# A two-layer decoder trunk in float32 on one core: the moves of transposed blocks by way of DRAM issued from GpSimd's queue instead of SP's

## The chip, the core and the metric

The kernel runs on one core of a Trainium2 chip. The core has TensorE (PE in the profile: matmuls, with PEld for the loading of weights into the array), VectorE (DVE), ScalarE (ACT), GpSimd (POOL) and SyncE (SP), which here does nothing but issue DMAs, and 16 DMA engines that all queues share. The metric is the time of one execution on the device in microseconds (us), the median of several runs.

## The reference

Two layers over 256 positions of width 2048, all in float32. Layer 0 mixes with retention heads and a gated linear recurrence, layer 1 with attention (16 heads), and each is followed by a gated MLP with a causal convolution of width 3 between up-projection and activation. Cut to what matters here:

```python
def conv_ffn(h, w_up, conv_w, conv_b, w_down):
    u = causal_dwconv(h @ w_up, conv_w, conv_b)
    gate, val = jnp.split(u, 2, axis=-1)
    return (jax.nn.gelu(gate) * val) @ w_down

for l in range(DEPTH):
    hn = rmsnorm(x, norm_mix[l])
    x = x + (even_mixer(hn, ...) if l % 2 == 0 else odd_mixer(hn, ...))
    x = x + conv_ffn(rmsnorm(x, norm_ffn[l]), ffn_w_up[l], ffn_conv_w[l], ffn_conv_b[l], ffn_w_down[l])
```

## The kernel before

**Weights in chunks.** Every projection is cut into blocks of 512 output columns, and a block into chunks of 256 rows, 512 KB each. There are 784 chunks. SP loads a chunk into one of four buffers `raw` (line 314), ScalarE copies it into `w_hi` (line 471), VectorE writes the remainder into `w_lo` (line 1099), and TensorE multiplies with both, so that float32 precision is kept. A load waits for `lo_ready` of the chunk four before it, ScalarE for the landing and for TensorE's end with the chunk four before (`chunk_used`). SP, ScalarE, VectorE and TensorE all walk through the same list of chunks; work between the chunks is placed by hand at a stage, the number of the chunk in the block behind which it stands.

**Blocks that come out transposed.** In most blocks TensorE computes positions by columns (`chunk_rows`, `chunk_values`: 12 matmuls a chunk, lines 837 to 839 and 855 to 857), while what follows needs columns by positions. VectorE transposes such a block from PSUM into `cross` in squares of 32 by 32 (`STREAM_TRANSPOSE`, two instructions: lines 1258 and 1259 in the up-projection, 1203, 1204, 1114, 1115, 1227 and 1547 elsewhere). The squares still have to change partitions. That is done by a move through DRAM: `put` writes `cross` in four pieces of 128 KB into `turn_line` (line 334, semaphore `put_out`), and `fetch` reads the 512 KB back into `h` (line 339, semaphore `moved`), once all four have landed. There are 69 such moves: 6 in the input projections of each layer, 3 in each output projection, 22 in each up-projection, 3 and 4 in the down-projections (the last four turn the residual x).

**The up-projection**, where 44 of the 69 are, has 22 blocks of 8 chunks in each layer, two to a turn (gate and value); the first turn stands apart, the other ten are a loop on every engine. For a block, VectorE transposes behind chunk 2 of the next block, waits for `moved` behind its chunk 7 and scales h (line 1265). ScalarE makes the first tap of the convolution behind chunk 0 of the block after that (line 534), VectorE the two others behind chunks 1 and 2 (lines 1272 and 1279), and then comes the transpose of the next block. `cross`, `turn_line` and `h` exist once, so one move must be over, and h be used up, before the next.

**Where the moves are issued.** All on SP, in the list of weight loads. In the up-projection `put` stands behind the load of chunk 6 and `fetch` behind the load of chunk 0 of the next block. In the input and output projections and the first layer's down-projection the places are like these, written out by hand. GpSimd loads a few constants at the start, the bias table once layer 0 is finished (line 445), and writes three of the four output blocks (line 449); it waits otherwise.

Of the kernel before, what the change touches and what calls it, by code (L numbers as in the profile page):

```python
# [21 lines left out]
P = 128  # L22
D = 2048
S = 256
# [3 lines left out]
NB = 512  # L28
BT = NB // P
CT = 2  # L30
RING = 4
# [6 lines left out]
PAIRS = D_FF // NB  # L38
SQ = 32
QUADS = P // SQ  # L40
OUTB = D // NB
ROWS = OUTB - 1
MOVED_QK = 3
# [4 lines left out]
HEADS, HEAD_DIM = 16, 128  # L48
# [22 lines left out]
MOVED_IN = (2, 3, 4, 5, 7, 8)  # L71
# [9 lines left out]
LAYER_TURNS = (INB * KC + OUTB * KC + 2 * PAIRS * KC + OUTB * FC) // RING  # L81
# [49 lines left out]
def build(nc, x_t, params, w_gates, rope, decay, rel_bias, buckets, identity,  # L131
# [3 lines left out]
    phases = (Phase(0), Phase(1))  # L135
# [63 lines left out]
    bias, _ = work("bias", [P, HEADS, S])  # L199
# [11 lines left out]
    bias_line = nc.dram_tensor("bias_line", (HEADS, 3 * P), F32, kind="Internal").ap()  # L211
# [27 lines left out]
    bias_loaded = sem("bias_loaded")  # L239
# [65 lines left out]
    def _(sp):  # L305
# [7 lines left out]
            src = w[bass.ds(rows * (CT * P), CT * P), cols].rearrange("(t p) n -> p t n", p=P)  # L313
            sp.dma_start(raw[:, s, :, :], src).then_inc(landed[s], 16)

        def put(n):

            sp.wait_ge(acc_drained, n + 1)
            write_quads()

        def put_x(k):

            sp.wait_ge(x_flipped, k + 1)
            write_quads()

        def put_qk(k):

            sp.wait_ge(qk_flipped, k + 1)
            write_quads()

        def write_quads():
            for i in range(QUADS):
                dst = turn_line[:, i, :].rearrange("(g c) n -> c g n", g=QUADS)
                sp.dma_start(dst, flip_quads[i * SQ:(i + 1) * SQ, :, :]).then_inc(put_out, 16)

        def fetch(k):

            sp.wait_ge(put_out, 16 * QUADS * (k + 1))
            sp.dma_start(h_quads[:, :, :], turn_line[:, :, :]).then_inc(moved, 16)

        for ph in phases:
            l = ph.layer
            for b, (_, _, col) in enumerate(ODD_BLOCKS if l else EVEN_BLOCKS):
                for c in range(KC):
                    if (l, b, c) == (0, 0, 0):
                        for u, landing in enumerate((tile_landed, landed[0])):
                            sp.dma_start(raw[:, 0, u, :], w_in[0][u * P:(u + 1) * P, col:col + NB]).then_inc(landing, 16)
                        continue
                    if (l, b, c) == (0, 0, 5):
                        sp.dma_start(par[:, 4 * KT:], params[:, 4 * KT:]).then_inc(const_loaded, 16)  # L350
                    load(w_in[l], ph.q_in + 2 * b, c, slice(col, col + NB), c)
                    if l and b >= 2 and b % 3 != 1 and b < 3 * MOVED_QK + 1:
                        k = 2 * ((b - 2) // 3) + (b % 3 == 0)
                        if c == 2:
                            put_qk(k)
                        if c == 4:
                            fetch(ph.m_in + k)
                    if l == 0 and b - 2 in MOVED_IN and c == 0:
                        fetch(MOVED_IN.index(b - 2))
                    if l == 0 and b - 1 in MOVED_IN and c == 6:  # L360
                        put(b - 1)
                    if (l, b) == (0, 0) and c in (1, 3, 4):
                        j = (1, 3, 4).index(c) + 1
                        part = slice(j * BT, (j + 1) * BT)
                        sp.dma_start(x_res[:, part, :], x_t[:, part, :]).then_inc(x_loaded[j], 16)
            for b in range(OUTB):
                for c in range(KC):
                    load(w_out[l], ph.q_out + 2 * b, c, slice(b * NB, (b + 1) * NB), MIX_ORDER[l][c])
                    if b >= 2 and c == 0:
                        fetch(ph.m_out + b - 2)  # L370
                    if b and c == 6:
                        put(ph.n_out + b - 1)
            for half in range(2):
                for c in range(KC):
                    load(w_up[l], ph.q_up + 2 * half, c, slice(half * D_FF, half * D_FF + NB), c)
                    if half == 0 and c == 0:
                        fetch(ph.m_up - 1)
                    if half and c == 6:
                        put(ph.n_up)
            with sp.Fori(1, PAIRS) as j:  # L380
                for half in range(2):
                    for c in range(KC):
                        load(w_up[l], ph.q_up + 4 * j + 2 * half, c, bass.ds(j * NB + half * D_FF, NB), c)
                        if c == 0:
                            fetch(ph.m_up + 2 * j + half - 2)
                        if c == 6:
                            put(ph.n_up + 2 * j + half - 1)
            for b in range(OUTB):
                cols = slice(b * NB, (b + 1) * NB)
                for c in range(FC) if b == 0 else DOWN_HEAD:  # L390
                    load(w_down[l], ph.q_down, FC * b + c, cols, c)
                    if b == 0 and c in (0, 8):
                        fetch(ph.m_down - 2 + c // 8)
                    if b == 0 and c == 6:
                        put(ph.n_down - 1)
                    if l and (b, c) == (0, 18):
                        put_x(0)
                    if l and (b, c) == (0, 20):
                        fetch(ph.m_down)
                    if l and b and c == 7:  # L400
                        put_x(b)
                    if l and b and c == 9:
                        fetch(ph.m_down + b)
                    if b and l == 0 and c == 6:
                        put(ph.n_down + b - 1)
                    if b and l == 0 and c == 8:
                        fetch(ph.m_down + b - 1)
                if b == 0:
                    continue
                with sp.Fori(*DOWN_TURNS) as t:  # L410
                    for i in range(RING):
                        load(w_down[l], ph.q_down + t, FC * b + i, cols, RING * t + i)
                for c in DOWN_TAIL:
                    load(w_down[l], ph.q_down, FC * b + c, cols, c)
# [7 lines left out]

    @block.gpsimd
    def _(pool):
        nc.gpsimd.memset(ones[:, :], 1.0).then_inc(consts_set, 1)

        pool.wait_ge(consts_set, 1)
# [11 lines left out]
        pool.dma_start(bias_line[:, :], line[0:HEADS, :]).then_inc(line_stored, 16)  # L439
        pool.wait_ge(line_stored, 16)  # L440

        pool.wait_ge(chunk_used, RING * LAYER_TURNS)

        hankel = bass.AP(bias_line.tensor, 0, [[1, P], [3 * P, HEADS], [1, S]])
        pool.dma_start(bias[:, :, :], hankel).then_inc(bias_loaded, 16)
        for b in range(OUTB - 1):

            pool.wait_ge(acc_drained, phases[1].n_down + b + 1)
            pool.dma_start(out_t[:, :, b * NB:(b + 1) * NB], x_nat[:, b, :, :]).then_inc(stored, 16)
        pool.wait_ge(stored, 16 * (OUTB - 1))  # L450


# [1305 lines left out]
```

## Time and profile before

| | us |
|---|---|
| median of three runs (2203.89 to 2205.47) | 2203.9 |
| the profiled execution | 2206.2 |
| its span, first to last instruction | 2204.3 |

| engine | busy us | share of the span |
|---|---|---|
| PE | 2197.0 | 100% |
| PEld | 1831.2 | 83% |
| DVE | 1509.0 | 68% |
| ACT | 1156.0 | 52% |
| POOL | 7.7 | 0% |

The granted clock of TensorE is 1.00 over the whole span. The DMA engines are busy for 71% of it and move 493 MB at 224 GB/s; 263808 of the 265777 packets come from SP's queue. Matmuls overlap in the profile: one has a duration of 0.39 us, and one begins every 0.23 us. So a pause of TensorE is read from the distance of two starts, not from the idle time alone.

### The profile page before, as it was taken

The page shows a single profiled execution, that of the slowest core. Times are in us where ns is not written, and L with a number is a line of the kernel's source. Part 1 is how long each engine was busy: PE and PEld are TensorE (multiplying, and loading weights), DVE is VectorE, ACT ScalarE, POOL GpSimd, SP SyncE. Part 2 cuts the span into 40 slices and gives each one's busy share as a digit, 9 for nine tenths or more (in the row PEclk, how much of TensorE's full clock was granted, in tenths as well). Part 3 has the DMA queues.
Part 4 walks back from the last instruction along what each step waited for, and adds up shares of the span by engine and source line. Part 5 has one row for each costly group of instructions (what it writes and reads, how often), then busy time and mean ns, then how long its engine had stood idle before and what let it go on. Part 6 is the DMA issues. An engine that isn't in the chain of part 4 may idle for free.

```text
span 2204.3 us, 28925 instructions
## 1 busy us (share of the span) xinstructions
PE 2197.0 (100%) x10046; PEld 1831.2 (83%) x10046; DVE 1509.0 (68%) x1923; ACT 1156.0 (52%) x1442; POOL 7.7 (0%) x17
## 2 busy tenths in 40 slices
PE   9999999999999999999999999999999999999999
PEld 8888888888888888888888888888888888888887
DVE  7877766777777776645566665576777777766444
ACT  6554455555655565444455555555555555554443
POOL 0000000000000000000000000000000000000000
PEclk9999999999999999999999999999999999999999
DMA  7766667777787777666676675567777777777664
GB/s 271 220 218 194 208 204 225 226 233 245 233 256 226 250 230 248 222 206 204 205 238 193 211 235 161 191 213 240 232 245 231 252 230 242 232 244 244 208 222 161
DMA packets 265777, 493.25 MB, mean 224 GB/s; under 512 B 18549, under 2 KB 53893, under 8 KB 265568
## 3 DMA queue, kind: packets, MB, share of 16 engines
q1 hardware_dynamic: 263808, 485.96, 70.5%
q0 software_dynamic: 1456, 5.65, 0.7%
q8 instruction: 51, 0.84, 0.2%
q10 hardware_dynamic: 432, 0.56, 0.1%
q14 instruction: 30, 0.25, 0.0%
HBM read 453.80 MB, written 38.30 MB: 223 GB/s over the span
## 4 chain that ended last, share of the span: by engine, by line
PE 80%; DMA 7%; DVE 6%; issue 3%; ACT 2%; SPq 1%; DVEq 0%; ACTq 0%
PE ps L855 15%; PE ps L856 15%; PE ps L857 15%; PE ps L837 8%; PE ps L839 8%; PE ps L838 8%; PE ps L814 6%; DMA h<-turn_line 5%; PE ps L818 3%; DMA turn_line<-cross 1%; DVE h L1265 1%; ACT w_hi L471 1%; DVE w_lo L1099 1%; DVE pad_g L1279 1%; DVE pad_g L1272 1%
## 5 line engine op out<-in xcount | busy, mean ns | idle before, releaser
L1099 DVE TENSOR_TENSOR w_lo<-raw,w_hi 128x1024 fp32r<-128x1024 f32 x783 | 948.4, 1223 | 561.5 <-ACT w_hi L471 535.1
L471 ACT ACTIVATE w_hi<-raw 128x1024 fp32r<-128x1024 f32 x783 | 813.9, 1056 | 680.8 <-PE ps L839 252.6
L855 PE MATMUL ps<-w_hi,xs 128*128 128x512 f32 x2048 | 799.0, 390 | 0.4 <-DVE w_lo L1099 0.4
L857 PE MATMUL ps<-w_hi,xs 128*128 128x512 f32 x2048 | 796.9, 389 | 0.0
L856 PE MATMUL ps<-w_lo,xs 128*128 128x512 f32 x2048 | 796.8, 389 | 0.0
L855 PEld LDWEIGHTS ps<-w_hi,xs 128*128 128x128 f32 x2048 | 384.4, 188 | 80.8 <-DVE w_lo L1099 1.3
L857 PEld LDWEIGHTS ps<-w_hi,xs 128*128 128x128 f32 x2048 | 384.4, 188 | 79.8
L856 PEld LDWEIGHTS ps<-w_lo,xs 128*128 128x128 f32 x2048 | 384.5, 188 | 79.1
L837 PE MATMUL ps<-w_hi,act 128*128 128x512 f32 x808 | 314.8, 390 | 1.0 <-DVE w_lo L1099 1.0
L838 PE MATMUL ps<-w_lo,act 128*128 128x512 f32 x808 | 314.4, 389 | 0.0
L839 PE MATMUL ps<-w_hi,act 128*128 128x512 f32 x808 | 314.4, 389 | 0.0
L837 PEld LDWEIGHTS ps<-w_hi,act 128*128 128x128 f32 x808 | 151.7, 188 | 32.7 <-DVE w_lo L1099 1.4
L839 PEld LDWEIGHTS ps<-w_hi,act 128*128 128x128 f32 x808 | 151.7, 188 | 31.6
L838 PEld LDWEIGHTS ps<-w_lo,act 128*128 128x128 f32 x808 | 151.7, 188 | 31.4
L814 PE MATMUL ps<-act,w_hi 128*128 128x512 f32 (+1 forms) x304 | 95.4, 395 | 0.0
L1265 DVE TENSOR_TENSOR h<-h,rstd 128x1024 f32<-128x1024 f32 x44 | 53.9, 1226 | 44.3 <-DMA h<-turn_line 43.4
L814 PE MATMUL ps<-xs,w_hi 128*128 128x512 f32 x256 | 80.9, 397 | 1.7 <-DVE w_lo L1616 1.3
L818 PEld LDWEIGHTS ps<-act,w_lo 128*128 128x128 f32 x304 | 57.1, 188 | 13.5
L542 ACT ACTIVATE act<-pad_v 128x1024 f32 (+1 forms) x22 | 23.4, 1063 | 80.1 <-DVE pad_v L1289 80.1
L534 ACT ACTIVATE pad_v<-h,par 128x256 f32<-128x256 f32 x88 | 45.8, 592 | 35.1 <-DVE h L1265 35.1
L818 PE MATMUL ps<-act,w_lo 128*128 128x256 f32 (+1 forms) x304 | 59.7, 278 | 0.0
L818 PEld LDWEIGHTS ps<-xs,w_lo 128*128 128x128 f32 x256 | 48.1, 188 | 11.3
(206 smaller groups left out, 1138.3 us busy)
## 6 DMA issues: line engine op xcount, KB each, us to landing
raw<-w_up SPq DMA_DIRECT2D x352, 512.0 KB, 4.6
raw<-w_in SPq DMA_DIRECT2D x191, 512.0 KB, 4.3
raw<-w_down SPq DMA_DIRECT2D x176, 512.0 KB, 4.6
turn_line<-cross SPq DMA_DIRECT2D x276, 128.0 KB, 2.5
h<-turn_line SPq DMA_DIRECT2D x69, 512.0 KB, 5.9
raw<-w_out SPq DMA_DIRECT2D x64, 512.0 KB, 4.6
bias<-bias_line POOLq DMA_DIRECT2D x1, 2048.0 KB, 11.0
x_res<-x_t SPq DMA_DIRECT2D x3, 512.0 KB, 7.2
```

Source lines behind the costliest of these rows:

```text
L471: act_f(w_hi[:, s, :, :], raw[:, s, :, :], ACT.Copy).then_inc(hi_ready, 1)
L534: ins = act_f(by_quad(pad[:, t, 0:S]), h_tiles[:, :, t, :], ACT.Identity, scale=w, bias=b)
L814: return mm(ps[:, 4 * group + m, :], w_hi[:, s, u, m * P:(m + 1) * P], rhs, start=first and u == 0, stop=False)
L818: return mm(ps[:, 4 * group + m, 0:S], w_lo[:, s, u, m * P:(m + 1) * P], rhs[:, 0:S], start=False, stop=last and u == CT - 1)
L837: mm(out, x_hi, w_hi[:, s, u, :], start=first and u == 0, stop=False)
L838: mm(out, x_hi, w_lo[:, s, u, :], start=False, stop=False)
L839: ins = mm(out, x_lo, w_hi[:, s, u, :], start=False, stop=last and u == CT - 1)
L855: mm(out, x_hi, w_hi[:, s, u, :], start=first and u == 0, stop=False)
L856: mm(out, x_hi, w_lo[:, s, u, :], start=False, stop=False)
L857: ins = mm(out, x_lo, w_hi[:, s, u, :], start=False, stop=last and u == CT - 1)
L1099: tt(w_lo[:, s, :, :], raw[:, s, :, :], w_hi[:, s, :, :].bitcast(F32), ALU.subtract).then_inc(lo_ready, 1)
L1265: tt(h_tiles, h_tiles, scale, ALU.mult).then_inc(normed, 1)
```

## The change

SP keeps the weight loads, three loads of x, the parameters and the last output writes. Its `put`, `put_x`, `put_qk`, `write_quads` and `fetch` move to GpSimd word for word, but for the engine. GpSimd gets a list of its own, in which each move is a wait for the transpose, four writes, a wait for `put_out` and the read. The bias table and the output writes are placed in that list. The other engines' programs are the same.

```diff
         def load(w, q, c, cols, rows):
...
-        def put(n):
-
-            sp.wait_ge(acc_drained, n + 1)
-            write_quads()
...
-        def fetch(k):
-
-            sp.wait_ge(put_out, 16 * QUADS * (k + 1))
-            sp.dma_start(h_quads[:, :, :], turn_line[:, :, :]).then_inc(moved, 16)
...
                 for half in range(2):
                     for c in range(KC):
                         load(w_up[l], ph.q_up + 4 * j + 2 * half, c, bass.ds(j * NB + half * D_FF, NB), c)
-                        if c == 0:
-                            fetch(ph.m_up + 2 * j + half - 2)
-                        if c == 6:
-                            put(ph.n_up + 2 * j + half - 1)
...
     @block.gpsimd
     def _(pool):
+        def put(n):
+
+            pool.wait_ge(acc_drained, n + 1)
+            write_quads()
...
+        def write_quads():
+            for i in range(QUADS):
+                dst = turn_line[:, i, :].rearrange("(g c) n -> c g n", g=QUADS)
+                pool.dma_start(dst, flip_quads[i * SQ:(i + 1) * SQ, :, :]).then_inc(put_out, 16)
+
+        def fetch(k):
+
+            pool.wait_ge(put_out, 16 * QUADS * (k + 1))
+            pool.dma_start(h_quads[:, :, :], turn_line[:, :, :]).then_inc(moved, 16)
...
-        pool.wait_ge(chunk_used, RING * LAYER_TURNS)
-
-        hankel = bass.AP(bias_line.tensor, 0, [[1, P], [3 * P, HEADS], [1, S]])
-        pool.dma_start(bias[:, :, :], hankel).then_inc(bias_loaded, 16)
-        for b in range(OUTB - 1):
-
-            pool.wait_ge(acc_drained, phases[1].n_down + b + 1)
-            pool.dma_start(out_t[:, :, b * NB:(b + 1) * NB], x_nat[:, b, :, :]).then_inc(stored, 16)
+        for ph in phases:
+            l = ph.layer
+            if l:
+                pool.wait_ge(chunk_used, RING * LAYER_TURNS)
+                hankel = bass.AP(bias_line.tensor, 0, [[1, P], [3 * P, HEADS], [1, S]])
+                pool.dma_start(bias[:, :, :], hankel).then_inc(bias_loaded, 16)
+                for k in range(2 * MOVED_QK):
+                    put_qk(k)
+                    fetch(ph.m_in + k)
+            else:
+                for k, b in enumerate(MOVED_IN):
+                    put(b)
+                    fetch(k)
+            for b in range(ROWS):
+                put(ph.n_out + b)
+                fetch(ph.m_out + b)
+            for j in range(PAIRS):
+                for half in range(2):
+                    put(ph.n_up + 2 * j + half)
+                    fetch(ph.m_up + 2 * j + half)
+            if l:
+                put_x(0)
+                fetch(ph.m_down)
+            for b in range(ROWS):
+                if l:
+                    put_x(b + 1)
+                    fetch(ph.m_down + b + 1)
+                    pool.wait_ge(acc_drained, ph.n_down + b + 1)
+                    pool.dma_start(out_t[:, :, b * NB:(b + 1) * NB], x_nat[:, b, :, :]).then_inc(stored, 16)
+                else:
+                    put(ph.n_down + b)
+                    fetch(ph.m_down + b)
```

SP's program in layer 0's up-projection loop, the kernel before: the loads of chunks 6, 7 and 0 and the move among them. (ISA and REGISTER_ALU are SP's own waits and address sums; a load is the row with `raw`.)

```order
L314 DMA raw<-w_up 128x2x512
L318 REGISTER_ALU
L334 DMA turn_line<-cross 32x4x256 [waits acc_drained]
L334 DMA turn_line<-cross 32x4x256 x3
L312 REGISTER_ALU
L314 ISA [waits lo_ready]
L314 DMA raw<-w_up 128x2x512
L312 ISA
L314 ISA [waits lo_ready]
L314 DMA raw<-w_up 128x2x512
L338 ISA
L339 DMA h<-turn_line 128x1024 [waits put_out]
```

The same place in the kernel after, on SP:

```order
L314 DMA raw<-w_up 128x2x512
L312 REGISTER_ALU
L314 ISA [waits lo_ready]
L314 DMA raw<-w_up 128x2x512
L312 ISA
L314 ISA [waits lo_ready]
L314 DMA raw<-w_up 128x2x512
```

Only the loads are left, each behind its own wait. On GpSimd in the kernel after, two moves of the same up-projection (the loop is written out there):

```order
L380 DMA turn_line<-cross 32x4x256 [waits acc_drained]
L380 DMA turn_line<-cross 32x4x256 x3
L385 DMA h<-turn_line 128x1024 [waits put_out]
L380 DMA turn_line<-cross 32x4x256 [waits acc_drained]
L380 DMA turn_line<-cross 32x4x256 x3
L385 DMA h<-turn_line 128x1024 [waits put_out]
```

Writes and read stand together there, with no load between them. The end of GpSimd's program after, in layer 1's down-projection:

```order
L380 DMA turn_line<-cross 32x4x256 [waits x_flipped]
L380 DMA turn_line<-cross 32x4x256 x3
L385 DMA h<-turn_line 128x1024 [waits put_out]
L432 DMA out_t<-x_res 256x1x512 [waits acc_drained]
L1689 UNCONDITIONAL_BRANCH [waits stored]
```

An output write, which had GpSimd's queue to itself, now stands behind a move.

## Rows read from the trace of the kernel before

**Rows 1.** The page's first part: busy time, share of the span, instructions.

```profile
PE 2197.0 (100%) x10046; PEld 1831.2 (83%) x10046; DVE 1509.0 (68%) x1923; ACT 1156.0 (52%) x1442; POOL 7.7 (0%) x17
```

**Rows 2.** Chain of waits, layer 1's up-projection: start us, us, what.

```profile
1571.60 0.68 DVE cross L1259
...
1573.64 2.70 DMA turn_line<-cross
1576.36 5.65 DMA h<-turn_line
1582.04 1.24 DVE h L1265
...
1592.80 0.69 DVE cross L1259
```

**Rows 3.** Busy time by stretch, layer 0's up-projection.

```profile
core 0: us, PE busy (x) PEld busy (x) DVE busy (x) ACT busy (x) POOL busy (x), PEclk, DMA share, GB/s
408.00:846.00 438.00, 438.00 (x1934) 362.68 (x1933) 328.58 (x403) 249.49 (x279) 0.00 (x0) 1.00 0.78 242
```

**Rows 4.** Instructions of line 1259, layer 0's and layer 1's up-projection.

```profile
L1259 DVE STREAM_TRANSPOSE cross<-ps x22: 672/673/675, 407.4 to 866.3; 128x512 f32<-128x512 f32 x22
...
L1259 DVE STREAM_TRANSPOSE cross<-ps x22: 672/674/676, 1505.8 to 1967.6; 128x512 f32<-128x512 f32 x22
```

**Rows 5.** Timeline of PE at two places: start us, us, what.

```profile
1880.17 0.39 PE L857 MATMUL ps<-w_hi,xs 128*128 128x512 f32 x1
1880.97 0.50 PE L855 MATMUL ps<-w_hi,xs 128*128 128x512 f32 x1 [0.42 <-DVE w_lo L1099]
...
1968.24 0.39 PE L839 MATMUL ps<-w_hi,act 128*128 128x512 f32 x1
1969.60 0.50 PE L837 MATMUL ps<-w_hi,act 128*128 128x512 f32 x1 [0.97 <-DVE w_lo L1099]
```

**Rows 6.** Timeline of SP, two moves in layer 1's up-projection.

```profile
1572.30 1.78 SPq L334 DMA_DIRECT2D turn_line<-cross  x4
...
1576.36 0.35 SPq L339 DMA_DIRECT2D h<-turn_line  x1
...
1593.50 1.78 SPq L334 DMA_DIRECT2D turn_line<-cross  x4
...
1598.05 0.36 SPq L339 DMA_DIRECT2D h<-turn_line  x1
```

**Rows 7.** Waits, whole run: total us, times, longest.

```profile
ACT w_hi L471 <- DMA raw<-w_up: 76.2, 41, 4.5
...
DVE h L1265 <- DMA h<-turn_line: 43.4, 36, 2.8
...
DVE h L1125 <- DMA h<-turn_line: 1.4, 2, 0.8
```

**Rows 8.** Timeline of GpSimd: two constant loads, one output write.

```profile
31.15 0.53 POOL L435 DMA_DIRECT2D decay_t<-decay  x1
31.67 0.53 POOL L436 DMA_DIRECT2D ident<-identity  x1
...
2107.01 0.69 POOL L449 DMA_DIRECT2D out_t<-x_res  x1 [59.16 <-DVE x_res L1689]
```

**Rows 9.** Timeline of VectorE around that output write.

```profile
2105.50 1.22 DVE L1689 TENSOR_TENSOR x_res<-x_res,ps 128x1024 f32<-128x1024 f32 x1
2107.03 1.23 DVE L1099 TENSOR_TENSOR w_lo<-raw,w_hi 128x1024 fp32r<-128x1024 f32 x1 [0.31 <-ACT w_hi L471]
```

**Rows 10.** DMA issues from 2040 to 2175 us: count, KB, us to landing.

```profile
raw<-w_down SPq DMA_DIRECT2D x50, 512.0 KB, 4.7
out_t<-x_res POOLq DMA_DIRECT2D x3, 512.0 KB, 5.1
turn_line<-cross SPq DMA_DIRECT2D x8, 128.0 KB, 3.5
```

**Rows 11.** The page's sixth part, DMA issues of the whole run.

```profile
turn_line<-cross SPq DMA_DIRECT2D x276, 128.0 KB, 2.5
h<-turn_line SPq DMA_DIRECT2D x69, 512.0 KB, 5.9
```

More of the change, by code:

```diff
@@ L314, in load @@
             sp.dma_start(raw[:, s, :, :], src).then_inc(landed[s], 16)
-        def put(n):
-            sp.wait_ge(acc_drained, n + 1)
-            write_quads()
[L321 to L334, printed above, removed]
-        def fetch(k):
-            sp.wait_ge(put_out, 16 * QUADS * (k + 1))
-            sp.dma_start(h_quads[:, :, :], turn_line[:, :, :]).then_inc(moved, 16)
         for ph in phases:
@@ L351, in _ @@
                     load(w_in[l], ph.q_in + 2 * b, c, slice(col, col + NB), c)
[L352 to L361, printed above, removed]
                     if (l, b) == (0, 0) and c in (1, 3, 4):
@@ L368, in _ @@
                     load(w_out[l], ph.q_out + 2 * b, c, slice(b * NB, (b + 1) * NB), MIX_ORDER[l][c])
[L369 to L372, printed above, removed]
             for half in range(2):
@@ L375, in _ @@
                     load(w_up[l], ph.q_up + 2 * half, c, slice(half * D_FF, half * D_FF + NB), c)
[L376 to L379, printed above, removed]
             with sp.Fori(1, PAIRS) as j:
@@ L391, in _ @@
                     load(w_down[l], ph.q_down, FC * b + c, cols, c)
[L392 to L407, printed above, removed]
                 if b == 0:
@@ L424, in _, with put_x, put_qk @@
     def _(pool):
+        def put(n):
+            pool.wait_ge(acc_drained, n + 1)
+            write_quads()
+        def put_x(k):
+            pool.wait_ge(x_flipped, k + 1)
+            write_quads()
+        def put_qk(k):
+            pool.wait_ge(qk_flipped, k + 1)
+            write_quads()
+        def write_quads():
[5 more added lines that the diff above has]
+            pool.dma_start(h_quads[:, :, :], turn_line[:, :, :]).then_inc(moved, 16)
         nc.gpsimd.memset(ones[:, :], 1.0).then_inc(consts_set, 1)
```

## The prediction

> **What bounds the kernel now.** I read the shares of the engines first. TensorE is busy for 2197.0 of 2204.3 us [rows 1], so nothing that shortens another engine can give much: all idle time of TensorE, the start included, is some 7 us. The question is therefore not what the change saves, but whether it makes TensorE wait, and where the margin is thinnest.
>
> That is the chain of waits in the second layer's up-projection. In one half turn of that loop (one block of 8 weight chunks) it goes from the second transpose on VectorE to the last write to DRAM, from its landing to the read, from there to the scaling of h, then through the convolution (ScalarE and VectorE in turn) to the next transpose, and never touches TensorE [rows 2]. Such a chain, where each block's transpose waits by way of the read for the block before, has a period of its own. Its parts: from the end of the transpose (1571.60 + 0.68 = 1572.28) to the start of the scaling (1582.04) is 9.76 us, which I call T; from there to the end of the next transpose (1592.80 + 0.69 = 1593.49) is 11.45 us, engine work that the change leaves alone. TensorE's side of the same block is 96 matmuls: 1934 of them took 438.00 us in a stretch without a stall, 0.2265 us each, so 21.74 us for a block [rows 3]. The chain keeps up while T is at most 21.74 - 11.45 = 10.29 us on average.
>
> How close is it? The second transpose of the 22 blocks starts from 407.4 to 866.3 us in layer 0 and from 1505.8 to 1967.6 us in layer 1 [rows 4]. Over 21 periods that is 21.85 and 21.99 us, both over 21.74: the chain already loses 0.11 and 0.25 us a block, 2.3 and 5.2 us a layer. In layer 0 TensorE never notices, because the split weights are ready a few us ahead. In layer 1 the lead runs out, and two starts of matmuls come late: 0.80 us after the one before at 1880.17 and 1.36 us at 1968.24, where 0.23 is usual, so 1.7 us of stall [rows 5]. The lead that was eaten is 5.2 - 1.7 = 3.5 us. That gives a rule for the kernel after: each layer stalls by 21 x (T - 10.29) - 3.5 us, where that is positive, and the kernel before has 1.7 us in all. T before is 10.40 and 10.54 us by the same periods.
>
> **The change part by part.** It takes 276 writes and 69 reads off SP and puts them on GpSimd's queue. Each of the 44 blocks of the two loops has four writes and one read; the other 25 blocks come later.
>
> What SP gains. It issued the four writes in 1.78 us, ahead of the next loads [rows 6]. These loads can now go as soon as VectorE has freed their buffers. ScalarE's waits on w_up loads, 76.2 us in the whole run [rows 7], should shrink. That is worth nothing to TensorE by itself: VectorE comes to its wait on the read earlier and then waits there, as it does already (43.4 us in 36 of 44 cases [rows 7]). In half of the blocks SP also held up the read itself: at 1593.50 + 4.55 = 1598.05 it came 0.5 us later behind its writes than the 4.06 us of the block at 1572.30 [rows 6]. That delay goes, -0.25 us on average.
>
> What GpSimd costs, term by term, as a new T (SP's value in brackets, [rows 2, 6]):
> - from VectorE's end to the first issue: GpSimd's out_t write came at 2107.01, VectorE's line 1689 ended at 2105.50 + 1.22 = 2106.72, so 0.29 us (0.02) [rows 8, 9].
> - three more issues: 31.15 to 31.67 is one pitch, 0.53, so 1.6 us (1.34) [rows 8]. Upper end 0.69 each, the out_t issue, so 2.1.
> - the last write's landing: no small write on this queue is in the trace. 512 KB took 5.1 us from GpSimd where SP's 512 KB loads took 4.7 in the same stretch [rows 10], 0.4 more. So 2.7 + 0.4 = 3.1 us (2.70). The writes now run beside a weight load that SP no longer holds back: writes landed in 3.5 us in the stretch where loads were under way, against 2.5 in the whole run [rows 10, 11], so between 0 and 1.0 more; I take 0.3, since only the first of the next loads is early enough.
> - the wait on put_out to the read's issue: 0.29 again (0.02), between 0.02 and 0.29.
> - the read: 5.1 us by out_t, the only transfer of its size from GpSimd in steady traffic, against 5.65 us for the read in the chain and 5.9 as a median [rows 2, 10, 11]. SP's read stands behind two 512 KB loads in SP's own queue, GpSimd's does not. Lower end 4.5 (0.6 below, the spread of SP's own), upper end 5.9.
> - to VectorE's start: 0.03, as before.
>
> The sum is 0.29 + 1.6 + 3.4 + 0.29 + 5.1 + 0.03 = 10.71 us. The low ends give 0.29 + 1.6 + 3.1 + 0.02 + 4.5 + 0.03 = 9.5, the high ends 0.29 + 2.1 + 4.1 + 0.29 + 5.9 + 0.03 = 12.7. With 10.71 a layer loses 21 x 0.42 - 3.5 = 5.3 us, two layers 10.6, against 1.7 now: +8.9 us. The profiled execution is 2206.2 us (span 2204.3), so it would be 2215.1; the median of the runs is 2.3 us lower, so the forecast is 2212.8, say 2213 us.
>
> The Trainium skill (DMA: Bandwidth & Descriptors, Issuing engines are not separate DMA queues) says that issuing from several engines only saves the issuing sequencer's time, as all transfers share the same DMA engines. By that rule the read would gain nothing by leaving SP's queue. With SP's 5.9 us for it, T would be 11.5 us and the loss about 42 us, 2246, which is inside my small loss; I give that end a third of the case's chance. The trace of before cannot settle it.
>
> The other 25 blocks (12 of the input projections, 6 of the output projections, 7 of the down-projections). Their consumers hardly wait: VectorE 1.4 us in 2 cases for the scaling of the input blocks [rows 7]. I cost them at nothing, covered by the stages between the transpose and its use; if T grew by 3 us there too, each could lose at most that, but the down-projection's lead is full when it comes. GpSimd's own older work moves behind the new waits: the bias table goes out once layer 0 is finished, after the last read of that layer, and the out_t writes each follow a read that is long done. The tail of the program is SP's, as before. Nothing here costs anything.
>
> **The rivals.**
>
> A, no measurable change: T stays at or below 10.60 us, where the rule gives 21 x 0.31 - 3.5 = 3.0 us a layer, 4.4 us above the kernel before. The mechanism is that leaving the queue of the weight loads pays for the slower issue: the read at 4.7 us or less, or its wait at 0.02 and the writes at 3.1, is enough, since my sum is only 0.11 above the point. For it: the low ends of three terms each do it alone. Against it: both new waits on GpSimd, 0.5 us together, are sure unless the second is quick. Time: 2202 to 2208, 2204 as the middle. This is the case on the other side of my forecast, and it decides at T = 10.60.
>
> B, a large loss: GpSimd prepares its transfers late because VectorE holds it off. right after a transpose it runs weight splits of 1.2 us each. If each of the five issues of a block had to wait for the end of an instruction, 0.4 us on average more than shown, T would be 12.7 and the kernel 2 x (21 x 2.41 - 3.5) - 1.7 = 92.5 us slower, 2296. Against it: the issues at 2107.01 and 31.15 took 0.69 and 0.53 us, the first beside a split of 1.23 us that began at 2107.03, and the three out_t transfers landed after 5.1 us as a median [rows 8 to 10]. But that row cannot show whether the 5.1 us holds such a wait.
> The Trainium skill (SBUF — State Buffer, the "DVE blocks DMA" trap) speaks of this: transfers from GpSimd starve while VectorE runs a copy-like instruction in its two-port modes, and two-input instructions only collide with GpSimd's reads. The loop has transposes and two-input instructions alone, so by that page B should not happen; no run here shows it yet.
>
> C, faster by over 0.2%: SP's earlier loads would have to bring more than 4.4 us. Only the 1.7 us of stall and some pieces at the start are there to be had, so I give it next to nothing.
>
> **How the numbers follow.** Small loss, T between 10.60 and 12.3 (2208 to 2280): 0.42, with 2213 as its value. A: 0.40. B or high ends together, above 2280: 0.16. C: 0.02. The smallest change that a measurement of this kernel can tell from none is about 0.2%, 4.4 us. So faster 0.02, same 0.40, slower 0.58. The range from 2200 (all stalls gone, 2203.9 - 1.7, and some run scatter) to 2280 (T = 12.3: 2 x (21 x 2.01 - 3.5) - 1.7 = 75.7 above) leaves out B and C's share, under 0.2.
>
> **What would show it.** In the profile after: the period of the loops' second transposes (21.74 if hidden, 11.45 + T if not); the chain's pieces from transpose to first issue, four issues, landing, read; VectorE's wait on the read, which should grow from 43.4 us; TensorE's waits on w_lo, a few us if I am right, nothing for A, tens for B; ScalarE's waits on weight loads, which should fall. A period at or under 21.8 us in both layers makes my forecast wrong, as does a period above 23.8.

## The result and the profile after

The kernel after takes 2302.6 us (median of five runs, 2301.43 to 2307.03) where the kernel before takes 2205.5 on the same chip. The ratio is 1.0446, with a 95% interval from 1.0435 to 1.0457, so the change costs 97 us. I had forecast 2213 with a range up to 2280. The sign was right, the size wrong by a factor of ten.

The first part of the page of the kernel after, the counterpart of [rows 1]:

```profile
PE 2227.0 (97%) x10046; PEld 1826.2 (79%) x10046; DVE 1506.1 (65%) x1923; ACT 1145.8 (50%) x1442; POOL 196.7 (9%) x362
```

The numbers of instructions of the four computing engines are unchanged. TensorE's share has fallen from 100 to 97% of a span of 2305.0 us, so the engine that hardly paused before now waits. Summed from the distances of its matmuls' starts (how is said below), its stalls are 103 us, where the kernel before has 7, and that is the whole loss. The waits of the whole run (total us, times, longest), to be set beside [rows 7]:

```profile
POOL h L385 <- DMA turn_line<-cross: 328.5, 68, 6.4
DVE h L1251 <- DMA h<-turn_line: 145.6, 44, 6.5
...
PE ps L841 <- DVE w_lo L1085: 64.2, 55, 2.9
...
DVE x_res L1197 <- DMA h<-turn_line: 24.7, 9, 6.6
...
ACT w_hi L457 <- DMA raw<-w_up: 117.7, 79, 4.2
```

VectorE waits for the read in each of the 44 blocks of the up-projections (145.6 us, it was 43.4), and TensorE waits for VectorE's weight splits (64.2, it was 0.4). A wait that was hardly there before stands at line 1197, the sum onto the residual in the output projections and layer 0's down-projection. ScalarE's waits on w_up loads were to shrink; this row rose from 76.2 to 117.7 us. ScalarE's other row on the same loads, which has no tile name in the view, fell from 40.2 to 26.7, so together they went from 116.4 to 144.4 us.

A small part of these 103 us is not waiting. TensorE's granted clock is 0.998 over the span because it stands at 0.50 (1.2 GHz instead of 2.4) in three stretches of 3.4 us, each at or just behind a stall of 2.4 to 3.0 us. The first, in layer 0's first turn of the up-projection, in the columns of [rows 3] (the stall ends at 395.5):

```profile
392.00:395.00 3.00, 0.64 (x3) 0.19 (x1) 2.93 (x4) 3.00 (x6) 0.00 (x0) 1.00 0.23 84
397.00:400.00 3.00, 3.00 (x8) 2.33 (x8) 3.00 (x10) 0.42 (x2) 0.00 (x0) 0.50 0.81 276
401.00:404.00 3.00, 3.00 (x15) 2.48 (x14) 2.85 (x4) 1.08 (x2) 0.00 (x0) 1.00 0.68 186
```

Matmuls start every 0.43 us there instead of every 0.23. 33 starts have that distance in the kernel after and 9 in the kernel before, so this costs some 5 of the 97 us (an estimate from 24 starts of 0.2 us each).

Where does a block's time go? The second transposes of the up-projections, as in [rows 4]:

```profile
L1245 DVE STREAM_TRANSPOSE cross<-ps x22: 673/673/675, 415.3 to 916.1; 128x512 f32<-128x512 f32 x22
...
L1245 DVE STREAM_TRANSPOSE cross<-ps x22: 673/673/674, 1566.6 to 2066.9; 128x512 f32<-128x512 f32 x22
```

The period is (916.1 - 415.3)/21 = 23.85 us in layer 0 and 23.82 in layer 1, against 21.74 us of TensorE's own work for a block. The chain of waits of one such block, with the places of [rows 2]:

```profile
1591.40 0.68 DVE cross L1245
1592.09 0.28 issue
1592.37 1.63 POOL turn_line L380 x3
1594.00 4.96 DMA turn_line<-cross
1598.96 0.28 issue
1599.24 4.75 DMA h<-turn_line
1604.01 1.24 DVE h L1251
...
1614.79 0.68 DVE cross L1245
```

T, from the end of the transpose (1592.08) to the scaling, is 11.93 us here, and from there to the end of the next transpose it is 11.46. Over all 44 blocks the means are: release 0.30, first to fourth issue 1.74, **fourth issue to the read's issue 5.19**, read to scaling 5.17, so T = 12.40 (10.45 before), and the rest of the chain 11.47 (11.47 before). The large piece is the landing of the fourth write. It took 2.70 us in [rows 2] and is 4.96 here. SP's timeline tells what stands beside it:

```profile
1593.59 7.75 SPq L314 DMA_DIRECT2D raw<-w_up  x5
```

SP issues the next weight load at 1593.59, 1.2 us behind GpSimd's first write (1592.37) and ahead of its fourth (1594.00). Before, the loads stood behind all four writes, at 1574.34 after a first write at 1572.30 [rows 6]:

```profile
1574.34 1.09 SPq L314 DMA_DIRECT2D raw<-w_up  x2
```

This holds throughout: at least one load is issued between the first and the fourth write in all 44 blocks of the up-projections after, and in none before.

In the experiments I give for each kernel the four numbers that matter: the fourth write's issue to the read's issue, the read's issue to the scaling, T, and R, the rest of the chain (means of the 44 blocks). Stalls of TensorE are summed from the distances of two starts of matmuls, less 0.23, wherever they are over 0.30 us. Where no interval is given a kernel ran once; beside it the kernel before took 2203.4 to 2205.7 us (medians). Differences of ten and more us can then be read, smaller ones not.

### The profile page after: what moved, and what is told of

It reads as the page before. It is cut to its first block, busy times and chain, and to the rows that moved or that the text cites. A ratio compares the mean times of both kernels' runs of the same rounds, so it can differ in the third digit from the quotient of the medians.

```text
span 2305.0 us, 28845 instructions
## 1 busy us (share of the span) xinstructions
PE 2227.0 (97%) x10046; PEld 1826.2 (79%) x10046; DVE 1506.1 (65%) x1923; ACT 1145.8 (50%) x1442; POOL 196.7 (9%) x362
## 2 busy tenths in 40 slices
DMA packets 239282, 493.26 MB, mean 214 GB/s; under 512 B 18549, under 2 KB 18565, under 8 KB 239072
## 4 chain that ended last, share of the span: by engine, by line
PE 45%; DMA 23%; DVE 14%; issue 8%; ACT 5%; POOL 4%; DVEq 1%; ACTq 1%
DMA h<-turn_line 12%; DMA turn_line<-cross 11%; PE ps L841 6%; PE ps L843 6%; PE ps L842 6%; PE ps L823 6%; PE ps L824 6%; PE ps L825 6%; PE ps L800 4%; POOL turn_line L380 4%; DVE h L1251 2%; ACT w_hi L457 2%; PE ps L804 2%; DVE pad_g L1265 2%; DVE pad_g L1258 2%
## 5 line engine op out<-in xcount | busy, mean ns | idle before, releaser
L457 ACT ACTIVATE w_hi<-raw 128x1024 fp32r<-128x1024 f32 x783 | 803.4, 1053 | 568.8 <-PE ps L825 213.2
L841 PE MATMUL ps<-w_hi,xs 128*128 128x512 f32 x2048 | 811.2, 396 | 64.8 <-DVE w_lo L1085 64.2
L380 POOL DMA_DIRECT2D turn_line<-cross x276 | 150.7, 553 | 1616.4 <-DVE cross L1245 770.3
L1251 DVE TENSOR_TENSOR h<-h,rstd 128x1024 f32<-128x1024 f32 x44 | 53.9, 1226 | 145.6 <-DMA h<-turn_line 145.6
L528 ACT ACTIVATE act<-pad_v 128x1024 f32 (+1 forms) x22 | 23.4, 1063 | 138.5 <-DVE pad_v L1275 138.5
L520 ACT ACTIVATE pad_g<-h,par 128x256 f32<-128x256 f32 x88 | 45.8, 591 | 63.5 <-DVE h L1251 63.5
```

The costliest lines, as they stand in the source:

```text
L380: pool.dma_start(dst, flip_quads[i * SQ:(i + 1) * SQ, :, :]).then_inc(put_out, 16)
L457: act_f(w_hi[:, s, :, :], raw[:, s, :, :], ACT.Copy).then_inc(hi_ready, 1)
L841: mm(out, x_hi, w_hi[:, s, u, :], start=first and u == 0, stop=False)
L1251: tt(h_tiles, h_tiles, scale, ALU.mult).then_inc(normed, 1)
```

## What makes the fourth write late: five kernels on one question

In the expectations, L is the theory that SP's loads, already under way, delay GpSimd's transfers. V is that VectorE's weight splits hold GpSimd off while it prepares them (my rival B), and P that each write costs GpSimd a preparation of its own, so that they queue behind each other.

**SP's next loads held until the writes have landed.** In the up-projections of the kernel after:

```diff
                         load(w_up[l], ...)
+                        if c == 6:
+                            sp.wait_ge(put_out, 16 * QUADS * (ph.m_up + 2 * j + half))
```

(SP's loop is written out here, since the wait counts on.)

> The changed kernel with the next weight loads held back: in the up-projections SP waits for put_out of the block's move before it issues the load of chunk 7 (SP's loop is written out for that, so that it waits on constants). In the changed kernel the time from the fourth write's issue to the read's issue is 5.2 us on average (I had 3.7 in the sum), T is 12.4. Theory L (GpSimd's transfers come late because weight loads issued meanwhile are ahead of them in the DMA engines): that time falls to 3.2 to 3.8 us. Theory V (VectorE's instructions hold off the preparation) and theory P (GpSimd prepares two transfers at once, and the third waits for the first to be over): it stays at 5.0 or more.

Measured: 2272.0 us, 31 us below the kernel after. The fourth write's issue to the read's is 3.13 us, where the kernel before has 3.04. GpSimd's timeline of one block:

```profile
1594.06 2.18 POOL L384 DMA_DIRECT2D turn_line<-cross  x4 [17.23 <-DVE cross L1249]
1598.63 0.56 POOL L389 DMA_DIRECT2D h<-turn_line  x1 [2.39 <-DMA turn_line<-cross]
```

In the kernel after the idle time before a read is twice as long:

```profile
1592.37 2.18 POOL L380 DMA_DIRECT2D turn_line<-cross  x4 [16.67 <-DVE cross L1245]
1599.24 0.56 POOL L385 DMA_DIRECT2D h<-turn_line  x1 [4.69 <-DMA turn_line<-cross]
```

So a write from GpSimd lands nearly as fast as one from SP when no load is in its way. VectorE does the same work meanwhile: in the first 5 us behind a move's first write it is busy for 80% in every other block and for 89% in the ones between, in this kernel as in the kernel after. Only the loads differ (in the first 3.6 us 1.2 and 3.0 of them after, 0 and 0.3 here), and the fourth write's issue to the read's falls from 5.07 and 5.32 us to 3.04 and 3.22 in the two kinds of block. That alone decides between L and V. T fell only to 11.14, because the read took 5.97 us (the held loads are issued just before it or beside it), and R rose to 12.00: the loads come late, and ScalarE waits 231.6 us for them instead of 117.7:

```profile
ACT w_hi L461 <- DMA raw<-w_up: 231.6, 66, 8.2
```

**The control: SP's loop written out, no wait.**

> Control for the held loads: the changed kernel with SP's up-projection loop written out, and no hold. If writing it out changes nothing: fourth write's issue to read's issue 5.2 us, T 12.4, time as the changed kernel's (2302 us). If that term falls under 4 us, it was the written-out loop and not the hold.

Measured: 2319.4 us, 5.36, 5.19, T 12.60, R 11.47. No part of the gain is there, so the gain of the run above came from the wait. Written out, the loop is even 17 us slower than the kernel after (one run; why was not followed up), so against its own control the hold gains 47 us.

**VectorE lightened.** In the up-projections' loops the splits of chunks 3 to 6 handle 128 columns of one half of a chunk instead of 1024 columns; this leaves out most of `w_lo` there.

```diff
-            tt(w_lo[:, s, :, :], raw[:, s, :, :], w_hi[:, s, :, :].bitcast(F32), ALU.subtract)
+            n = P if light else NB
+            u = slice(0, 1) if light else slice(0, CT)
+            tt(w_lo[:, s, u, 0:n], raw[:, s, u, 0:n], w_hi[:, s, u, 0:n].bitcast(F32), ALU.subtract)
```

> The changed kernel with VectorE nearly idle behind the transpose: in the loops of both up-projections the subtraction for w_lo of chunks 3 to 6 covers 128 of 1024 columns, so the output uses stale remainders there. Theory V: with 0.3 instead of 1.2 us instructions in the way, fourth write's issue to read's issue falls from 5.2 to under 4 us in the blocks that have no other VectorE work there (every other one), and T to about 11. Theories L and P: 5.0 or more, T as before at 12.2 or more.

Measured: 2342.0 us, slower by 39 us; 5.75, 5.42, T 13.20, R 11.47. With less work on VectorE the writes land later, not sooner. The mean hides two kinds of block that take turns: 6.57 us and 4.92. Theory V had named the blocks in which VectorE has only the shortened splits as the quick ones. One of each kind, GpSimd's rows, SP's loads in the 3.6 us from the first write, and VectorE's busy time in the 6.5 us from it (stretch and its length, VectorE's busy time and instructions, granted clock, DMA share, GB/s):

```profile
1608.78 2.19 POOL L380 DMA_DIRECT2D turn_line<-cross  x4 [16.08 <-DVE cross L1247]
1617.00 0.56 POOL L385 DMA_DIRECT2D h<-turn_line  x1 [6.03 <-DMA turn_line<-cross]
...
1609.07 2.86 SPq L314 DMA_DIRECT2D raw<-w_up  x4
...
1608.78:1615.28 6.50, 1.49 (x5) 1.00 0.82 251
```

```profile
1633.47 2.18 POOL L380 DMA_DIRECT2D turn_line<-cross  x4 [15.91 <-DVE cross L1247]
1639.69 0.56 POOL L385 DMA_DIRECT2D h<-turn_line  x1 [4.04 <-DMA turn_line<-cross]
...
1633.76 1.95 SPq L314 DMA_DIRECT2D raw<-w_up  x2
...
1633.47:1639.97 6.50, 4.24 (x7) 1.00 0.80 258
```

The slow block has VectorE busy for 1.49 us and four loads; the quick one has it busy for 4.24 us and two loads. Over all 44 the slow kind has 3.9 loads in those 3.6 us, the other 2.0. V is refuted, and the order is the one that L asks for: VectorE frees the buffers sooner, so the first load is issued 0.35 us behind the first write (1.20 in the kernel after), and the more loads, the later the landing.

**Half the load.** The loads of the up-projections' loops bring 256 KB instead of 512; the other half of each buffer keeps old data.

```diff
-            sp.dma_start(raw[:, s, :, :], src).then_inc(landed[s], 16)
+            sp.dma_start(raw[:, s, 0:part, :], src).then_inc(landed[s], 16)
```

> The changed kernel with half the weight traffic: in the loops of both up-projections each load brings only the first 256 KB of its chunk (the other half of the buffer is left as it was, so the output is another). Theory L: fourth write's issue to read's issue falls from 5.2 to about 4 us, the read to VectorE's start from 5.2 to about 4.5. Theories V and P: the first stays at 5.0 or more.

Measured: 2248.4 us; 4.51, 4.49, T 11.04, R 11.47. Less load traffic, earlier landing, as L says, though the first term fell by only 0.7 us, where I had expected 1.2.

**Eight writes of 64 KB instead of four of 128 KB.**

```diff
+                for e in range(2):
+                    part = slice(e * SQ // 2, (e + 1) * SQ // 2)
+                    pool.dma_start(dst[part], flip_quads[...]).then_inc(put_out, 16)
```

> The changed kernel with each of the four writes cut in two (8 of 64 KB, 16 partitions each). The issues take 7 x 0.54 = 3.8 instead of 1.6 us. Theory P (pairs, each waiting for the one before to be over, some 2 us): last write's issue to read's issue grows to 6 us or more, T to 15 or more. Theory L: the last write's issue to the read's issue stays at 5.0 us or falls a little, since the loads in its way are older by then; T about 14. Theory V: like L, 5 us.

Measured: 2403.1 us. From the last issue to the read's it is 4.91 us, not more than 5.19, and T grew to 14.24: the issues take 3.82 us instead of 1.74, and the other terms hardly move. One block (single ones lie between 3.3 and 7.1 us; this is one of the longer):

```profile
1624.46 4.05 POOL L382 DMA_DIRECT2D turn_line<-cross  x8 [39.13 <-DVE cross L1247]
1633.88 0.56 POOL L387 DMA_DIRECT2D h<-turn_line  x1 [5.37 <-DMA turn_line<-cross]
```

P, in the form that it has above, is refuted as well: it asked for 6 us or more, and the run of held loads had already brought the term to 3.13 with GpSimd's four writes as they are. What a further issue costs is its 0.55 us pitch.

## Which part of the change costs what

**The 44 moves of the up-projections against the 25 others.** Each part alone on GpSimd, the other left on SP (each queue with semaphores of its own):

```diff
+    put_up, moved_up = sem("put_up"), sem("moved_up")
...
-            for j in range(PAIRS):
-                for half in range(2):
-                    put(ph.n_up + 2 * j + half)
-                    fetch(ph.m_up + 2 * j + half)
```

> The kernel before, with the 25 moves outside the up-projections (input, output and down-projections) issued from GpSimd and the 44 of the up-projections left on SP. The prediction costed these 25 at nothing. If that holds: 2205 us, within 0.2%, with the stalls of the loops as before (0 and 1.0 us). The trace of the kernel after shows some 10 us more of stalls outside the up-projections than before (input and output projections +5, down-projections +5), part of which may come from the up-projection's chain that was late: if the 25 moves cost by themselves, 2209 to 2215. The other 44 would then be worth the rest of the 97 us. If the loops stall here too, their loss isn't from the moves of the loops alone.

Measured, with the 25 on GpSimd: 2227.1 us, ratio 1.0101 (1.0087 to 1.0115), so 21.4 us where I had costed nothing. The up-projections' loops are as before (T 10.44, stalls 0.3 and 0 us). The stalls stand elsewhere: 5.9 and 6.9 us in the first turns of the up-projections, right behind the output projections' last move (0.1 before), 6.0 and 3.2 in layer 0's input and layer 1's output projections (3.1 and 0.4 before). Some 1.5 us of the 6.0 are from the first 20 us of the program, before any move (3.9 us of stalls there, 2.5 before), so no effect of the change. In each of the two first turns one pause of 3.0 us stands, and right behind it TensorE's granted clock is 0.50 for 3.4 us, which is some 1.6 us of the 5.9 and of the 6.9. VectorE's timeline in layer 0's output projection, this kernel's and then the kernel before's:

```profile
368.66 0.67 DVE L1222 STREAM_TRANSPOSE cross<-ps 128x512 f32<-128x512 f32 x1
...
381.65 1.29 DVE L1229 TENSOR_TENSOR x_res<-x_res,h 128x512 f32<-128x512 f32 x2 [3.49 <-DMA h<-turn_line]
```

```profile
361.92 0.67 DVE L1204 STREAM_TRANSPOSE cross<-ps 128x512 f32<-128x512 f32 x1
...
373.68 1.29 DVE L1211 TENSOR_TENSOR x_res<-x_res,h 128x512 f32<-128x512 f32 x2 [0.21 <-DMA h<-turn_line]
```

From the transpose's end to the sum it was 11.1 us with a wait of 0.21. It is 12.3 now with a wait of 3.49, and the splits behind it come late.

> The other half of the split: the 44 moves of the up-projections on GpSimd, the 25 others on SP as before. If the two parts add up, the loss is that of the kernel after (97 us) less that of the 25 moves alone (21 us): 76 us, 2281, with loops that stall 36 to 38 us each as in the kernel after, T 12.4 us, and the first turns of the loops (6.1 and 7.5 us after) back at 0.1. Rival: the 25 moves lengthen only the start of a chain that is late anyway, and the parts do not add: 2290 to 2303. A T well below 12.4 would mean that something besides the queue of the move itself sets it.

Measured, with the 44 on GpSimd: 2281.1 us, ratio 1.0337 (1.0320 to 1.0355), so 76.5 us. The stalls of the loops are 34.9 and 33.0 us, those of their first turns 0.1 each, T is 12.27. Together 21.4 + 76.5 = 97.9, against 97.1 for both: the parts add.

## Can a part of it be kept?

**The writes on SP, only the reads on GpSimd.**

```diff
         def fetch(k):
-
-            sp.wait_ge(put_out, 16 * QUADS * (k + 1))
-            sp.dma_start(h_quads[:, :, :], turn_line[:, :, :]).then_inc(moved, 16)
+            pass
...
+        def fetch(k):
+
+            pool.wait_ge(put_out, 16 * QUADS * (k + 1))
+            pool.dma_start(h_quads[:, :, :], turn_line[:, :, :]).then_inc(moved, 16)
```

> One half of the change: the 276 writes stay on SP at their old places, the 69 reads go from GpSimd's queue. Theory L (only what is issued behind weight loads comes late): the writes go out before the next loads as in the kernel before, 1.34 + 2.9 us, and the read behaves as in the changed kernel, 5.2 us; with 0.03 for the first issue and nothing lost on SP's order T is 9.3 to 9.7, under the 10.29 that TensorE allows, so no stall in the loops and a time of 2201 to 2204 us: same, at best 0.1% faster. Rival (GpSimd's transfers are slow by themselves, reads too): T over 10.6, slower by 0.3% or more.

Measured: 2251.9 us, ratio 1.0206 (1.0189 to 1.0223), with 3.00, 6.61, T 10.98, R 12.04. A miss. The writes are as before, but the read takes 6.61 us instead of 6.04, and SP's loads, which no longer wait for the writes' landing, are issued beside it. Both the read and ScalarE's work come late. ScalarE's two waits on w_up loads, 76.2 and 40.2 us before, are:

```profile
ACT w_hi L491 <- DMA raw<-w_up: 118.8, 71, 5.3
ACT L491 <- DMA raw<-w_up: 67.9, 20, 4.6
```

**The same, with SP waiting where its read stood.**

```diff
+                        if c == 0:
+                            sp.wait_ge(put_out, 16 * QUADS * (ph.m_up + 2 * j + half - 1))
```

> The kernel with only the reads on GpSimd (2251.9 us, T 10.98, scaling to next transpose 12.04), with SP's wait on put_out put back where the read stood (SP's loop is written out for it). If the loss there came from the load that SP now issues before the read can go: the read to VectorE's start falls from 6.6 to about 5.6, T to about 10.2, scaling to transpose back to 11.5, and the time to 2205 to 2215 us. If it comes from the read taking turns with the two loads already under way, whatever follows: no change, 2240 us or more.

Measured: 2242.7 us; 3.14, 6.32, T 10.83, R 11.91. The expectation's second branch came true, so the lost wait on SP is not the main cause. How large its part is this run does not tell: 9 us is less than single runs can show, and SP's loop is written out here, which by itself cost 17 us in the control above. What is left as the cause is that the read and the loads are under way at once from two queues; that is argued from the order of the issues and has no run of its own.

**Two writes on each queue.**

```diff
-            for i in range(QUADS):
+            for i in range(2):          # SP, semaphore put_sp
...
+            for i in range(2, QUADS):   # GpSimd, semaphore put_out
```

> Of the four writes, the first two are SP's at their old place (semaphore put_sp), the last two are GpSimd's (put_out); the read is GpSimd's. Both queues issue at once, so GpSimd's two are out 0.8 us behind the transpose, before the next loads have their data under way. Theory L: GpSimd's last write to the read's issue 3.3 us or less (5.2 in the changed kernel), T = 0.3 + 0.54 + 3.3 + 5.2 = 9.3 us, time 2201 to 2204 us. Rival (a write from GpSimd takes long in any case): 4.5 to 5.2 us, T over 10.6, slower.

Measured: 2279.5 us, ratio 1.0344 (1.0321 to 1.0367); GpSimd's last write to the read 4.57, read 6.56, T 11.97, R 11.47. A miss: halving the issues saves GpSimd a microsecond, but its two writes go out while SP's two are under way and just before the next load. By the records of the packets the first write from GpSimd had data under way 1.87 us after its issue, where the first write of a move in the kernel after needs 1.16.

**All on SP, the read one load earlier.** The kernel before, with the read behind the load of chunk 7:

```diff
-                        if c == 0:
-                            fetch(ph.m_up + 2 * j + half - 2)
...
+                        if c == 7:
+                            fetch(ph.m_up + 2 * j + half - 1)
```

> The kernel before, all moves on SP, with the read one place earlier in the up-projections: behind the load of chunk 7 instead of behind the load of chunk 0 of the next block. Theory O (what counts is the order in which loads and moves reach the DMA engines, and SP's one queue keeps it): the read goes 4.06 us behind the first write in every block (4.06 and 4.55 before) and has one 512 KB load ahead of it, not two, so it lands 1 us or more sooner; T falls from 10.45 to 9.2 to 9.8 on average, under 10.29, the loops' period is 21.75, and the 1.7 us of stall at the end of layer 1's loop are gone: 0.0 to 0.1% faster, the same within what can be measured. Rival: the held load of chunk 0 (issued 4.4 us behind the transpose instead of 2.6 to 3.9) lands too late for ScalarE, the path from the scaling to the next transpose grows from 11.47 to over 12 us, and the kernel is slower by 0.3% or more.

Measured: 2220.4 us, ratio 1.0069 (1.0056 to 1.0083); 2.72, 5.17, T 9.27, but R 12.92. The rival came true. T fell below the 10.29 that I had named as the limit, and the kernel still became slower, since R grew by 1.45 us. By the order of SP's program the load of chunk 0 now waits until the read has gone, and ScalarE waits longer for loads: 67.3 us in one of its two rows (40.2 before), and in the other, where it was 76.2:

```profile
ACT w_hi L473 <- DMA raw<-w_up: 151.2, 64, 4.2
```

No version that I ran beats the kernel before. Whether the moves would fare better on a second queue other than GpSimd's, ScalarE's for one, was not tried.

## Why the prediction was wrong, step by step

**What bounds the kernel: right.** TensorE had no slack, and the chain from transpose to transpose was the thin place. With R unchanged at 11.47, the rule "21 x (T - 10.29) - 3.5 us a layer" comes within 5 us in five kernels. For the 44 moves alone (T 12.27) it gives 2 x 38.1 - 1.7 = 74.5 us; measured 76.5. For the halved loads (T 11.04) it gives 22.8, and 44.2 with the 21.4 of the other moves; measured 44.9. For the lightened VectorE (T 13.20) it gives 113.5, and 134.9 so; measured 138.5. For the kernel after (T 12.40) it gives 79.9, and 101.3 with the other moves; measured 97.1. For the written-out loop (T 12.60) 88.3 and 109.7; measured 113.8. With eight writes (T 14.24) it gives 157.2 and 178.6, but 199.7 were measured. There the 25 other moves have eight writes too and cost more than 21.4 (the stalls outside the loops sum to 48 us, 27 in the kernel after), and the granted clock is 0.50 in 13 stretches of 3.4 us instead of three. The rule also fails where R moves, as in the read one load earlier. I had called R "engine work that the change leaves alone". For this change that was so, but R holds ScalarE's wait on loads, and a change to the loads' order changes it.

**The sum for T: the third term was wrong.** Release 0.29, measured 0.30. Three pitches 1.6, measured 1.74. The last write's landing and the wait behind it, 3.1 + 0.3 + 0.29 = 3.7 us, measured 5.19. The read 5.1 + 0.03, measured 5.17. Of the 1.69 us by which T came out above 10.71, 1.5 are this one term, over the 42 periods 63 of the 97 us. With the 21.4 us below and the 8.9 that were forecast that is 93; the smaller terms bring the rule to 101, and 97 were measured. T 12.40 alone puts the time at 2284 us, above my range, and the periods of 23.85 and 23.82 us are just over the 23.8 that I had named as the sign of being wrong. My prediction said "writes landed in 3.5 us in the stretch where loads were under way", and then took 0.3 of the 1.0 us "since only the first of the next loads is early enough". In those rows the writes still stood in SP's queue ahead of the loads behind them. The new case, a load issued between GpSimd's first and fourth write, was in no row. I had noted that the writes "now run beside a weight load that SP no longer holds back" and should have seen that no row bounded it from above. At the high end of all terms, T 12.7, the rule gave 2296, and to that I gave 0.16.

**The other 25 blocks at nothing: wrong, 21.4 us.** The cover I named was "the stages between the transpose and its use". The row that I took for all of them (VectorE's 1.4 us at line 1125) is of the input projections. In the output projections VectorE already waited 0.21 us for the read, so there the margin was nil. The kernel that has these moves alone on GpSimd shows what they cost.

**What SP gains: wrong in sign.** The next load does go out sooner, 1.20 us behind the first write instead of 2.02. A w_up load also lands no later than before (4.6 us as a median in both kernels). Yet ScalarE's two rows of waits on these loads grew from 116.4 to 144.4 us. My guess, which no run tests: a load can be issued only when VectorE has split the chunk four before it, and VectorE now stands still for 145.6 us at its wait on the read.

**The read leaving SP's queue: the number right, the mechanism not shown.** From issue to scaling it takes 5.17 us, against 6.04 before; I had 5.13. My reason was that it leaves two loads of its own queue behind. But with the reads alone on GpSimd, beside SP's loads, it takes 6.61 us, and on SP with one load ahead instead of two it takes 5.17 as well. So the queue alone does not set it, what is in flight does, and the hit is in part luck. The Trainium skill (DMA: Bandwidth & Descriptors, Issuing engines are not separate DMA queues) says that issuing from several engines only saves the sequencer's time for the issue, so the read would gain nothing by leaving. These runs show more than that, and in both directions: 5.17 and 6.61 us against 6.04.

**Rival B: the size nearly right, the mechanism refuted.** It named T 12.7 and 2296; T is 12.40. But it had VectorE hold GpSimd off, and with a lighter VectorE T grew, while with VectorE as busy as ever and the loads held the writes landed early. The Trainium skill (SBUF — State Buffer, the "DVE blocks DMA" trap) says that GpSimd cannot write its descriptors while VectorE runs an instruction in a two-port mode, which a float32 copy within SBUF brings about. The loops have no such copy on VectorE, so by that page nothing should be held off, and the lightened kernel agrees: T 13.20 against 12.40.

**What stays open.** That loads under way delay a GpSimd write is shown from both sides (held, 3.13; half the size, 4.51; as they come, 5.19; more and sooner, 5.75). At what point of its path the write waits, in the preparation of its descriptors or for its turn at the DMA engines, is not. The records of the packets narrow it: the first write has data under way 1.16 us after its issue with the loads as they come and 1.15 with them held, so its start is not delayed. But from 2.5 to 4.5 us behind that issue only 31 of a move's 192 packets begin in the kernel after, against 172 of SP's queue, where with the loads held it is 105 against 7 (means of the 44 blocks).

## What to carry to other kernels

In this kernel the program order of SP's one queue acted as a priority: with the writes ahead of the next loads their landing took 3.04 us with the wait behind it, and 5.19 from a second queue with a load between them. Before moving small, urgent transfers off a queue of large, patient ones, read from the timeline which large ones are issued within a few microseconds of them, and bound the landing by a row in which both are in flight from different queues; if there is none, the upper bound is open and the chances should say so. And price each group of moved instructions by its own consumer's wait: a wait of 0.2 us in the trace is the sign that there is no margin.

## What the runs showed of the hardware

A write of 128 KB from GpSimd's queue took 2.7 us to land in the kernel that holds SP's loads back in the up-projections, and 4.5 us in the kernel after, as medians of all 276. In that order:

```profile
turn_line<-cross POOLq DMA_DIRECT2D x276, 128.0 KB, 2.7
```

```profile
turn_line<-cross POOLq DMA_DIRECT2D x276, 128.0 KB, 4.5
```

SP's own took 2.5 before [rows 11]. The slower landing is thus for the most part no property of the queue. What belongs to GpSimd's queue is 0.3 us from a semaphore to the issue (0.03 on SP), and a pitch of 0.54 us as a median, 0.58 as a mean, instead of 0.45. The same bytes also went in fewer packets, 239282 instead of 265777, and that brought nothing that could be seen.
